# A build-time planner that reckons each kind of DMA with its own rate, in a hybrid RG-LRU and attention block on eight cores

## The reference, cut to what matters

```python
h = rms_norm(x, norm1_g)
lru_x, lru_gate, q, k, v = split(h @ w_in)              # w_in 1024 x 2560, five parts of 512
lru_x = causal_dwconv(lru_x)                            # width 4
r, i  = sigmoid(block_diag(lru_x, wa)), sigmoid(block_diag(lru_x, wx))
a     = exp(-8 * r * softplus(-lam));  u = sqrt(1 - a*a) * (i * lru_x)
out_a = gelu(lru_gate) * scan(a, u)                     # h[t] = a[t] * h[t-1] + u[t]
out_b = diff_attention(q, k, v)                         # 4 heads, two softmax maps each, chunk-causal
x = x + concat(out_a, out_b) @ w_out                    # 1024 x 1024
gate, val = split(rms_norm(x, norm2_g) @ w_up)          # 1024 x 6144
x = x + (gelu(causal_dwconv(gate)) * val) @ w_down      # 3072 x 1024, conv of width 3
return rms_norm(x, final_norm_g)
```

## Time and profile before

| what | us |
|---|---|
| runs: median of three | 1937.38 |
| runs: lowest, highest | 1807.07, 2090.08 |
| the profiled execution | 1812.31 |
| its span on the slowest core (core 6) | 1810.8 |
| spans of the eight cores | 1797.9 to 1810.8 |
| TensorE busy (11456 matmuls) | 1695.0 |
| VectorE, ScalarE, GpSimd busy | 1223.7, 1070.8, 421.5 |

### The profile page before, as it was taken

The page is one execution under the profiler, slowest core; times in us unless marked ns, Lnnn a source line. Parts: engine busy times, 40 slices in busy tenths (PEclk is TensorE's granted clock), DMA queues, the critical chain, the costliest instruction groups (busy, mean ns, idle before and its releaser), DMA issues.

```text
span 1810.8 us, 35688 instructions; the slowest of 8 cores (1797.9 to 1810.8 us)
## 1 busy us (share of the span) xinstructions
PE 1695.0 (94%) x11456; PEld 854.3 (47%) x11456; DVE 1223.7 (68%) x2040; ACT 1070.8 (59%) x1412; POOL 421.5 (23%) x665
## 2 busy tenths in 40 slices
PE   4768898899999999999999999999999999999997
PEld 1334443345554555544444454445554555544343
DVE  2675987449785496755977397836967378765844
ACT  5764786447863578734674377634885368932601
POOL 0331732005321041211511043201302023211400
PEclk9868999999999999999999999999999999999999
DMA  9994699968874634455656466445355354544644
GB/s 280 287 283 144 188 314 279 317 230 266 240 243 159 208 132 151 166 181 198 207 180 206 141 210 212 147 159 201 127 192 191 107 184 156 174 150 153 224 149 140
DMA packets 113399, 356.50 MB, mean 197 GB/s; under 512 B 10816, under 2 KB 11072, under 8 KB 113088
## 3 DMA queue, kind: packets, MB, share of 16 engines
q1 hardware_dynamic: 113216, 354.21, 59.7%
HBM read 294.40 MB, written 59.77 MB: 196 GB/s over the span
## 4 chain that ended last, share of the span: by engine, by line
PE 71%; DMA 12%; issue 6%; DVE 5%; ACT 3%; POOL 2%; SPq 0%; DVEq 0%; ACTq 0%; POOLq 0%
PE pb L815 35%; PE pb L833 25%; PE pb L1043 5%; PE pb L1001 3%; DMA KT<-w_in 3%; DMA ringF<-wslab 2%; DMA facc<-w_down 2%; DMA ringA<-wslab 1%; DMA KT<-w_up 1%; PE pb L788 1%; DMA Va<-w_up 1%; DVE aT L909 1%; ACT raw L892 1%; DMA Va<-w_out 1%; DVE facc L909 1%
## 5 line engine op out<-in xcount | busy, mean ns | idle before, releaser
L815 PE MATMUL pb<-hT,ringF 128*128 128x512 bf16 x3072 | 708.0, 380 | 17.0 <-DMA ringF<-wslab 6.0
L815 PEld LDWEIGHTS pb<-hT,ringF 128*128 128x128 bf16 x3072 | 287.7, 98 | 349.9 <-issue 35.0
L833 PE MATMUL pb<-ringF,aT 128*128 128x512 bf16 x1536 | 354.6, 383 | 4.2 <-ACT ringF L742 3.5
L1030 ACT ACTIVATE PT<-pb,prm 128x1024 bf16<-128x1024 f32 (+1 forms) x288 | 295.6, 1062 | 67.5 <-DVE pb L1023 25.1
L801 POOL TENSOR_TENSOR sm<-sm 128x1 f32<-128x1 f32 (+1 forms) x128 | 99.2, 777 | 793.8 <-DVE sm L798 782.9
L815 PE MATMUL pb<-hT,ringA 128*128 128x512 bf16 x1024 | 248.1, 391 | 17.2 <-DVE ringA L743 7.4
L833 PEld LDWEIGHTS pb<-ringF,aT 128*128 128x128 bf16 x1536 | 147.5, 98 | 176.3 <-issue 13.2
L1171 DVE TENSOR_TENSOR xf<-pb,xf 128x512 f32<-128x512 f32 x192 | 131.9, 688 | 125.6 <-PE pb L833 122.4
L1156 DVE TENSOR_TENSOR aT<-pb,aT 128x512 bf16<-128x512 f32 x192 | 129.9, 684 | 91.4 <-PE pb L815 76.2
L1043 PE MATMUL pb<-Va,PT 128*128 128x129 bf16 x2176 | 175.9, 222 | 13.3 <-DVE acp L850 5.6
L1043 PEld LDWEIGHTS pb<-Va,PT 128*128 128x128 bf16 x2176 | 145.9, 99 | 82.7 <-issue 33.5
(11 more groups left out here) (120 smaller groups left out, 1783.6 us busy)
## 6 DMA issues: line engine op xcount, KB each, us to landing
ringF<-wslab SPq DMA_DIRECT2D x240, 512.0 KB, 4.6
ringA<-wslab SPq DMA_DIRECT2D x98, 512.0 KB, 5.5
xr<-x SPq DMA_DIRECT2D x64, 512.0 KB, 8.1
KT<-w_up SPq DMA_DIRECT2D x36, 512.0 KB, 7.5
Va<-w_up SPq DMA_DIRECT2D x36, 512.0 KB, 7.7
wslab<-ringF SPq DMA_DIRECT2D x36, 512.0 KB, 6.3
x<-xr SPq DMA_DIRECT2D x32, 512.0 KB, 4.0
xf<-x SPq DMA_DIRECT2D x32, 512.0 KB, 8.7
```

Source lines behind the costliest of these rows:

```text
L815: last = e.matmul(bank(p), lhsT=w[:, kk, cc * 128:(cc + 1) * 128], rhs=src[:, hf * 4 + kk, :], start=(hf == 0 and kk == 0), stop=(hf == 1 ...
L833: last = e.matmul(bank(p), lhsT=src[:, k0 + hf * 4 + kk, t * 128:(t + 1) * 128], rhs=w[:, kk, :], start=(hf == 0 and kk == 0), stop=(hf == ...
L1030: last_exp = op("act", act_us(2 * wid, ptr=1), lambda e, s=s, pt=pt, wid=wid, h=h: e.activation(out=PT[:, pt.s, :, 0:wid], in_=psum[:, s.s ...
```

## The change

Nothing is computed in another way and no instruction is added or left out. The planner's numbers change:

- each DMA of the SP queue is reckoned by its tag: 262e3 bytes per us for a float32 weight load, 308e3 for a load of x, 290e3 for the parameters, 220e3 for the staged small weights, 370e3 for all others (loads and writes of bfloat16 slabs, writes of x1 and of the output) where it was 310e3 for all;
- an issue holds SP for 0.7 us (float32 weight loads) or 0.45 us, where it was 0.4 us;
- the queue starts with 2.0 us of transfers in it;
- the table `FR` of where each stage stands relative to its group gets other numbers in eight of its nine entries (F1 stays): B and A stand earlier, C earlier, F2 and L a little later.

```diff
+RATE = {"ldw": 262e3, "ldx": 308e3, "prm": 290e3, "stg": 220e3}
...
-        line = {"sp": 0.0, "pool": 0.0}
+        line = {"sp": 2.0, "pool": 0.0}
...
-                line[e] += n.dma / bw[e]
+                line[e] += n.dma / (bw[e] if e == "pool" else RATE.get(n.tag, 370e3))
                 n.fin = max(t, line_t) + 0.6 + line[e] + min(line[e], line[other]) + 1.6
-                free[e] = t + (hold if e == "pool" else 0.4)
+                free[e] = t + (hold if e == "pool" else 0.7 if n.tag == "ldw" else 0.45)
...
-        FR = dict(N=(-0.393, -0.251), A=(-0.183, -0.035), F1=(-0.034, 0.330), G=(0.324, 0.340), F2=(0.391, 0.664), F3=(0.693, 1.033), L=(0.429, 0.623), B=(-0.130, 0.496), C=(0.679, 0.968))
+        FR = dict(N=(-0.445, -0.247), A=(-0.289, -0.127), F1=(-0.034, 0.330), G=(0.279, 0.358), F2=(0.420, 0.693), F3=(0.695, 1.033), L=(0.443, 0.637), B=(-0.160, 0.430), C=(0.603, 0.898))
```

## The result

The changed kernel takes 1822.12 us (median of 12 runs, 1816.59 to 1825.73), the kernel before 1813.22 us on the same chip. The ratio is 1.0071, with an interval of 1.0058 to 1.0085: slower by some 13 us, where 1805 was forecast against 1812 before. The time lies in the range of 1784 to 1834, but on the other side of the kernel before. In some executions a pair of cores, or a die, has a mean clock some hundredths lower than the rest, so beside each ratio stands the median span of the cores whose die stayed at 0.975 or more ("quiet cores": 1801.0 to 1801.8 us for the kernel before in every comparison, 1808.8 for the changed one).

What follows compares the result with a forecast made beforehand. Weights bound the first 360 us, TensorE the other 1440. Gains of 3.7 us up to F1(0) and 3.7 at A(2), 0 for the later groups, make 7.4 off 1812.3: 1805 us, range 1784 to 1834.

Steps and rivals of the forecast that it cites:

- First and second place: End of B(0), and C(0) to F1(0): 1.9 and 3.1 us sooner, F1(0) starts 5.0 us earlier, net gain 3.7 us.
- Third place: F2(0) to A(2): A(2) can begin 10.7 us sooner, 7.0 us of F3(0) matmuls now follow it, net gain 3.7 us.
- six DMAs of 1.79 us: A(2) stands behind the twelfth load of `w_down` instead of the sixteenth, so it can begin 10.7 us sooner.
- Rival (a): The start gains nothing, bytes bound from 220 us on: 1812 us; chance 0.25, shared with the rival of unchanged queue order.
- the term for the other seven groups: Everything behind the start: 0 gained, bounds 11 us won and 22 us lost, from 21.7 us of TensorE idle time.
- rival (c): Ring shared by F3 and F1: waits for slabs at seven passages, 44 us, 1849 us; 0.12 with other losses there.
- Rival (b): Queue moves faster from 220 to 370 us, 313 GB/s: 9.5 us less, 1795 us; 0.08 with other later gains.
- The order of the queue: At F2(0)'s last slab: by ring order alone, three loads moved ahead cost 5.4 us, a net loss of 1.7 us.

Runs made afterwards that it cites:

- The runs at 310: Changed kernel with slab loads, writes and other DMAs reckoned at 310e3 instead of 370e3, run twice: ratios to before 1.0024 and 1.0073, quiet cores 1799.8 and 1800.8 us.
- 290: Changed kernel with slab loads, writes and other DMAs reckoned at 290e3 instead of 370e3: ratio to before 0.9987, quiet cores 1799.4 us.
- the run at 230: Changed kernel with slab loads, writes and other DMAs reckoned at 230e3 instead of 370e3: ratio to before 1.0131, quiet cores 1823.2 us.
- the one with the writes alone: Changed kernel with only the writes reckoned at 310e3, slab loads left at 370e3: ratio to before 1.0104, quiet cores 1814.3 us.

## Why the prediction was wrong

**First and second place: right, and undersized.** Head 3's values in one run and the shorter way to F1(0) were forecast at 1.9 and 5.0 us; on the two profiled cores C(0) came 10.2 and F1(0) 13.2 us earlier, and over all cores the lead is 8.8 us at 150 us of work, where the terms sum to 3.7. The forecast took only the moves at these places, while the order differs ahead of them too: the lead is 4.2 us already at 60 us of work, before the end of B(0). What the two moves gave by themselves, no run separates.

**Third place: right on two cores, wrong over all.** A(2) begins at 338.72 (forecast 338), as "six DMAs of 1.79 us" had it. On the two profiled cores TensorE has done 229.3 us of its work there, before it had done 236.2: 14.8 us earlier with 6.9 us less done, 7.9 us ahead where the sum said 7.4. But that is partly luck: core 6 of the kernel before, whose times the forecast took, is the latest of its eight cores at 260 us of work. Over all cores the lead falls from 8.8 us at 150 us of work to 1.7 at 260. The step did not look at F2(0) between the second and the third place: three waits of 2.30, 1.98 and 2.61 us, each with a stretch at half clock behind it, are in no term. Rival (a) had the right end of this, that "every wait removed there has a second one close behind it"; its reason, that the bytes bound, does not hold there: the DMA engines idle in that stretch, at 0.85, and the lead in bytes shrinks with that of TensorE.

**The failing step is the term for the other seven groups.** "I take 0" was reasoned from the idle time of the order before, which can hardly shrink; that a changed order can add waits stood only in the bounds (up to 22 us lost) and in rival (c). Measured: 9.9 us more idle time after 360 us on the profiled cores, and over all cores 7.1 us lost behind 260 us of work (from 1.7 us ahead to 5.4 late). Of the 12.8 us between the 7.4 forecast and the 5.4 lost, these are 7.1; the other 5.7 are missing at the end of F3(0). Rival (c) had the mechanism, a ring whose next slab cannot be loaded in time, and the wrong ring: `ringF` behind F3, where the waits shown went from 6.0 to 3.7 us. It was `ringA`, of the output projection and L, 0.8 to 8.7, and with it the exponents of the attention. What the forecast did not ask is which of the planner's clocks sets the distance between a load and its use; the rate of 370e3 for slabs was in the diff, and against its 1.42 us for a load in a queue the trace of the kernel before has 1.6 between two landings. The runs at 310 (by the quiet cores) and 290 show that with this table the time after group 0 hangs on that rate. That it does so by way of the margin of the slabs is argued from waits A; the run at 230 and the one with the writes alone show that it isn't the whole of it.

**Rival (b).** The queue did not move faster: 280 GB/s instead of 293 from 220 to 370 us.

**The order of the queue.** The row at 626.41 above shows a slab load that lands 11.13 us after its issue, behind six other DMAs. The Trainium skill (DMA: Bandwidth & Descriptors, Queues, rings and completion order) says that an engine consumes its ring's descriptors in order; the long landing fits that rule, but does not by itself show it. The prediction weighed the order of the queue for the start alone, and it bore on the later groups. What made the difference here is not which DMAs stand ahead, since before they are the same six and the load lands after 6.2 us, but in which order they stand and how soon behind them it is issued.

## What to carry to other kernels

A planner that is told a lone transfer's rate is right where a load goes alone; in a queue that is shared with writes and other loads it lands later (1.6 us behind the load ahead instead of 1.42), and the planner can set the use of a buffer too early. Give it what the traces have under load, and change the number in steps: here 290 lost nothing, and 230 lost 1.3%. And where an order is planned as a whole, a forecast of the places that win is half of it: ask, for every stretch behind them, what work no longer covers its chains.

## What had not been expected of the hardware

Three waits of 1.98 to 2.61 us in F2(0), behind full work, left TensorE at the lower of its two levels for a while (1.2 instead of 2.4 GHz): the eight matmuls behind the first two take 3.37 and 3.13 us instead of 1.89 (rows at 268.41, 281.14 and 338.72), so that each of these waits costs more than 3 us. The granted clock of 270:315 is 0.91 with these waits in it or just ahead. But the length of a wait does not decide it alone: the 2.56 us ahead of F3(0), at 306.42, left the clock as it was, for the sixteen matmuls behind it take 3.61 us, under twice 1.89. So did the 0.81 us ahead of F1(0), at 169.46: its twelve matmuls take 2.75 us.
